# The gate product of the third head in the second mixer loop, moved behind its value products

## What is computed

```
def _mix(h, l, prm, past):
    proj = h @ prm['w_in'][l]
    hq, hf, hi, hg, sq, sk, sv, mx, mo, ga, gb, gc = jnp.split(proj, _in_split_points(), axis=-1)
    ...
    o_a, S_new = _hgrn2(hq, hf, hi, hg, lb, S0, prm['hg_gain'][l], hg_chunk)
    ...
        o_b = _sb_attend(q, jnp.concatenate([pk.astype(k.dtype), k], axis=1),
                         jnp.concatenate([pv.astype(v.dtype), v], axis=1),
                         P + jnp.arange(T), jnp.arange(P + T), sbb)
    ...
    o_c, (C_new, n_new, m_new, buf_new) = _mlstm(mx, mo, buf0, l, prm, C0, n0, m0, ml_chunk)
    merged = (jax.nn.sigmoid(ga.astype(f32)) * (o_a @ prm['w_hg_proj'][l])
              + jax.nn.sigmoid(gb.astype(f32)) * (o_b @ prm['w_sb_proj'][l])
              + jax.nn.sigmoid(gc.astype(f32)) * (o_c @ prm['w_ml_proj'][l]))
    y = (merged @ prm['w_out'][l]).astype(h.dtype)

def _mlstm_chunk(carry, inp):
    logD = b[:, :, None, :] - b[:, None, :, :] + it[:, None, :, :]
    m_t = jnp.maximum(b + m[:, None, :], jnp.max(logD, axis=2))
    Dm = jnp.exp(logD - m_t[:, :, None, :])
    W = jnp.einsum('bthd,bshd->btsh', q, k) * Dm
    numer = (inter[..., None] * jnp.einsum('bhvd,bthd->bthv', C, q)
             + jnp.einsum('btsh,bshv->bthv', W, v))
    denom = inter * jnp.einsum('bhd,bthd->bth', n, q) + jnp.sum(W, axis=2)
    ...
```

## Time and profile before

| | us |
|---|---|
| median of 3 runs | 1796.72 (1793.66 to 1801.37) |
| the profiled execution's own time | 1797.36 |
| its span | 1795.6 |
| TensorE busy | 1712.5 (95% of the span) |
| VectorE busy | 1035.5 (58%) |
| ScalarE busy | 789.3 (44%) |
| TensorE waiting for ACT L2017 at L1003 | 4.3 in two waits |
| TensorE waiting for pages at L757 | 1.6 (`pages`) and 1.1 (`ring`) |
| mean granted clock of TensorE | 0.984 |

### The profile page before, as it was taken

One profiled execution on the slowest core, in us unless ns is written; L12 is line 12 of the kernel. 1 busy time (PEld: TensorE's weight loads), 2 busy tenths in 40 slices (PEclk: granted clock), 3 DMA queues, 4 the chain that ended last, 5 costly groups with the idle time before them and its releaser, 6 DMA issues.

```text
span 1795.6 us, 33082 instructions
## 1 busy us (share of the span) xinstructions
PE 1712.5 (95%) x12604; PEld 1490.7 (83%) x12604; DVE 1035.5 (58%) x1874; ACT 789.3 (44%) x1430; POOL 71.1 (4%) x103
## 2 busy tenths in 40 slices
PE   5999999999999999999979999999999999999998
PEld 3898988878876687999969889788778766879997
DVE  3554545675567656655455554465665765566554
ACT  2554544445333315665345554353444331256552
POOL 0000000000000000000000000100000100000000
PEclk7999999999999999999999999999999999999999
DMA  8778565555557825555657784665464686455451
GB/s 340 260 260 329 210 224 205 183 209 220 190 210 259 314 97 210 186 176 205 253 194 277 268 334 170 234 227 185 148 241 154 236 316 218 143 210 187 171 219 56
DMA packets 85802, 391.81 MB, mean 218 GB/s; under 512 B 12328, under 2 KB 17712, under 8 KB 55344
## 3 DMA queue, kind: packets, MB, share of 16 engines
q1 hardware_dynamic: 72520, 368.15, 55.8%
q10 hardware_dynamic: 13160, 22.02, 3.5%
HBM read 377.30 MB, written 12.83 MB: 217 GB/s over the span
## 4 chain that ended last, share of the span: by engine, by line
PE 80%; DVE 9%; DMA 4%; ACT 3%; issue 2%; SPq 1%; ACTq 1%; POOL 0%; POOLq 0%; DVEq 0%
PE ps L594 17%; PE ps L589 15%; PE ps L590 15%; PE ps L550 10%; PE ps L776 3%; PE ps L794 3%; PE ps L793 3%; PE ps L570 2%; PE ps L740 2%; PE ps L658 1%; DMA pages<-in_k_pages 1%; PE ps L757 1%; PE ps L556 1%; DMA ring<-in_w_ffn_in 1%; DVE ring_parts L1137 1%
## 5 line engine op out<-in xcount | busy, mean ns | idle before, releaser
L1137 DVE TENSOR_TENSOR ring_parts<-ring,pages_parts 128x1024 fp32r<-128x1024 f32 (+1 forms) x288 | 334.0, 1193 | 158.9 <-ACT pages_parts L1753 158.8
L589 PE MATMUL ps<-arena_parts,pages_parts 128*128 128x264 f32 x1536 | 392.2, 290 | 18.3 <-DVE xn_parts L1225 10.2
L1753 ACT ACTIVATE pages_parts<-ring 128x1024 fp32r<-128x1024 f32 (+1 forms) x288 | 285.1, 1027 | 183.8 <-DMA ring<-in_w_ffn_in 55.7
L590 PE MATMUL ps<-xn_parts,pages_parts 128*128 128x264 f32 x1408 | 356.5, 287 | 0.0
L589 PEld LDWEIGHTS ps<-arena_parts,pages_parts 128*128 128x128 f32 x1536 | 294.3, 192 | 36.9 <-issue 30.5
L590 PEld LDWEIGHTS ps<-xn_parts,pages_parts 128*128 128x128 f32 x1408 | 268.9, 191 | 0.0
L594 PE MATMUL ps<-arena_parts,ring_parts 128*128 128x264 f32 x1536 | 225.7, 287 | 0.0
L550 PE MATMUL ps<-xn,ring 128*128 128x264 f32 x896 | 208.9, 389 | 0.6 <-ACT xn L1760 0.6
L594 PEld LDWEIGHTS ps<-arena_parts,ring_parts 128*128 128x128 f32 x1536 | 205.9, 190 | 0.0
L550 PEld LDWEIGHTS ps<-xn,ring 128*128 128x128 f32 x896 | 166.2, 190 | 34.9 <-ACT gates L1867 3.5
L590 PE MATMUL ps<-gates_parts,pages_parts 128*128 128x264 f32 x704 | 176.3, 285 | 0.0
(11 more groups left out here) (352 smaller groups left out, 2493.6 us busy)
## 6 DMA issues: line engine op xcount, KB each, us to landing
ring<-in_w_ffn_in SPq DMA_DIRECT2D x88, 1024.0 KB, 5.1
ring<-in_w_ada SPq DMA_DIRECT2D x32, 1536.0 KB, 6.5
ring<-in_w_a SPq DMA_DIRECT2D x32, 1536.0 KB, 6.9
ring<-in_w_ffn_down SPq DMA_DIRECT2D x32, 1408.0 KB, 6.2
pages<-in_k_pages SPq DMA_DIRECT2D x128, 256.0 KB, 6.0
ring<-in_w_ada SPq DMA_DIRECT2D x24, 1024.0 KB, 6.7
pages<-in_v_pages SPq DMA_DIRECT2D x88, 256.0 KB, 6.3
ring<-in_w_proj SPq DMA_DIRECT2D x8, 1536.0 KB, 8.2
```

Of the source, the lines that this page charges most:

```text
L589: mm(ps[:, b, 0:T], tile, hi[:, k, :], start=start, stop=False)
L590: return mm(ps[:, b, 0:T], tile, lo[:, k, :], start=False, stop=False)
L1137: v.tensor_tensor(ring_lo[:, r, at * P:(at + n) * P], w, whi[:, place, 0:n * P].bitcast(F32), ALU.subtract)\
L1753: A(whi[:, place, 0:n * P], ring[:, r, at * P:(at + n) * P], ACT.Copy).then_inc(S.whi_ready, 1)
```

## The change

The tuple that places the gate products changes for the third head (i = 2): product 5 moves from `FIRST_GATE` to `SECOND_GATE`, and the call for the first place gets the condition that the second had. ScalarE's program reads the same tuples, so its evacuation moves with it.

```
-FIRST_GATE, SECOND_GATE = (None, 3, 5, 6), (2, 4, None, 7)
+FIRST_GATE, SECOND_GATE = (None, 3, None, 6), (2, 4, 5, 7)
...
                 for i in range(HEADS):
                     if i:
                         key_rows(i)
-                        gslot = next_gate(FIRST_GATE[i], gslot)
+                        if FIRST_GATE[i]:
+                            gslot = next_gate(FIRST_GATE[i], gslot)
                         value_half(4 * i)
```

## The result

The changed kernel takes 1808.82 us (median of 4 runs, 1806.47 to 1809.04) against 1796.97 us before (4 runs, 1793.66 to 1801.37). The ratio is 1.0057, with a 95% interval of 1.0034 to 1.0081. Beside the experiments it was run again, and 9 to 12 us over the kernel before were expected: 1807.62 us, ratio 1.0059 (1.0040 to 1.0079). The forecast was 1801.4 us, the range ended at 1807. The sign of the forecast's sum was right, its size was half of what came.

What follows compares the result with a forecast made beforehand. TensorE, busy 1712.5 of 1795.6 us, was taken as the bound, so order matters only where it waits or its clock falls. Layer losses of 2.5 and 2.2 us (+4.7) on 1796.72 gave 1801.4 us, range 1796 to 1807.

Steps and rivals of the forecast that it cites:

- the queue: SyncE's queue: w_proj[1] waits for the gate product, half 12 starts 9.3 us after its issue; layers lose 2.5 and 2.2 us.
- The local part: TensorE, third head: gap before L1003 filled, but bare waits for pages and VectorE; first layer's head ends 0.7 us later.
- rival 1: Half 12's pages are in time, only TensorE's reordering counts: -1.7 us for both layers, 1795.0 us; 8%.
- The clock: TensorE's granted clock may fall behind the new waits, 1.5 us per fall; kept out of the sum, 28%.
- the rival with three falls: Far end of the 28% rival: one to three clock falls on TensorE give 1803 to 1806 us.
- the sign that the prediction itself had named for being wrong: Both layers' loops together change by less than 2 or more than 9 us.
- Rival 3: SyncE's queue: w_proj[1] and pages behind it move slowly (9.7 us), half 12 another 3.1 us later per layer, 1807.6 us; 10%.

Runs made afterwards that it cites:

- e3_held_proj: Kernel before, gate product in its old place, with w_proj[1] held until the third head's sum of squares (L1003): ratio 1.0052 to the kernel before.
- e1_late_proj: Changed kernel with w_proj[1] issued behind the pages of half 13 in place of half 11: ratio 0.9998 to the kernel before.
- e4_filled: Changed kernel with unread filler matmuls, 14 in front of half 8 and 20 in front of half 12: ratio 1.0050 to the kernel before.
- e4b_filled_short: Changed kernel with unread filler matmuls, 8 in front of half 8 and 11 in front of half 12: ratio 1.0037 to the kernel before.
- e6_both_late: Changed kernel with w_proj[0] issued behind the pages of half 8 and w_proj[1] behind those of half 13: ratio 0.9979 to the kernel before.

## Why the prediction was wrong

**What bounds the kernel, and the queue.** Right. That the gap before L1003 is filled and yet nothing is won, that w_proj[1] holds the pages of half 12 back, and that this is the main cost, is what the traces and e3_held_proj show. Its term was 9.3 us from issue to half 12. The runs have 9.30 and 9.39 us in the first layer and 9.96 and 10.03 us in the second: right, and 0.7 us short in the second layer.

**The local part.** Right in its sum, in the first layer partly by luck. Decay products 5.3 us (first layer) and 5.2 us (second) behind L1003 were forecast; they came at 4.81 and 5.32 us. In the first layer the waits were forecast as 0.9 us for pages and 1.8 us for VectorE and came as 1.89 and 0.27 us: half 8 came later than thought, and GpSimd's instruction began 2.4 us behind the second head's L1004, where it was 3.2 us behind L1003 before, so that VectorE was held up earlier and behind the wait for pages. In the second layer the wait for pages was 2.60 us, where 2.7 was forecast. The part on its own was priced in rival 1 at -0.8 and -0.9 us, and e1_late_proj has -0.8 and -0.9 us.

**The clock: the step that failed.** The sum left the falls of the clock out. The new waits were seen and their lengths too (2.7 and 3.3 us), but because the one old gap of 2.16 us had brought a fall in one layer and none in the other, the prediction called a fall a toss-up, made it a rival with 28%, and summed the forecast without any. That does not follow from its own reading: if each of three or four new waits of such a size is a toss-up, no fall at all has a chance of one in eight or less. In fact they came at the same three places in both profiles of the changed kernel: behind 3.26 and 3.35 us of waiting at half 12 in the first layer, behind 2.60 and 2.93 us at half 8 in the second, and behind 3.92 and 3.99 us at half 12 there. Only the wait of 1.89 (1.82) us at half 8 in the first layer brought none. The prices: 14.72 - 13.19 = 1.5 us behind half 12 in the first layer and 14.59 - 13.19 = 1.4 us in the second (both against the stretch in e4_filled and e4b_filled_short), and at the decay products 1480.36 - 1476.00 = 4.36 us to the query rows against 2.71 us before, 1.7 us. Together 4.6 us, where the sum had nothing.

The forecast's 4.7, the 4.6 us of the clock and the 0.7 us of the pages make 10.0 us; the two loops have 9.8 and 10.4. Layer by layer, and without the falls, the first lost 3.53 - 1.5 = 2.0 us (2.5 in the forecast) and the second 6.30 - 3.05 = 3.25 us (2.2 in the forecast). With 9.8 us for the two together, the sign that the prediction itself had named for being wrong, over 9 us, came. So the rival with three falls was what happened, priced about right at 1.5 us each and given too small a chance. The range ended at 1807 because it took three falls as its far end, and with that had no room for slower pages in the same run.

**The rivals.** Rival 3, slower transfers by 3.1 us in each layer, did not come: w_proj[1] took 6.5 and 7.2 us, not 9.7. Rival 1 needed pages that are not held, and e1_late_proj built just that.

**The chances.** Slower by over 0.5% had 8%. Both measurements lie at 0.57 and 0.59% with intervals from 0.34 to 0.81%, so on either side of that bound.

## What to carry to other kernels

When work moves on one engine, look for the load that waits for its end: a queue issues in order, so everything behind that load moves too, and here this cost 10 us where the move alone made no difference that could be measured. Give a new wait of TensorE like those here, of 2.6 to 4.1 us, the price of the half clock behind it in the sum itself and not in a rival, and ask before filling a gap whether the place that the work comes from can stand bare: with one load out of the way the move was worth nothing, and with both the kernel was 3.8 us faster. How far a load is moved matters too: two halves further back, that gain was gone.

## What was not expected of the hardware

- Over all kernels here the granted clock fell to half behind 11 of the 12 waits of 2.60 us and more in these loops; the exception is one of 3.15 us in e3_held_proj's second layer. A stretch at half clock had ended 2 us before that wait, but the wait of 3.04 us in its first layer had one 2.6 us before it, and there the clock fell again; why the two differ is open. Behind 2.37 us in e1_late_proj it did not fall. In e4b_filled_short it fell with no wait of note in the 9 us before. Of the old gap of 2.16 us before L1003 there are eight in the four kernels that keep it, and the clock fell behind four. So a wait of about 2 us may or may not cost 1.5 us more, with the same order of work.
- VectorE is held up by GpSimd for what is left of GpSimd's instruction: a tensor_scalar of 0.28 us took 1.92 us, a tensor_tensor of 0.43 us took 2.01 us. Both read SBUF alone. VectorE's instructions with an operand in PSUM were not held up: the tensor_tensor in front of the two tensor_scalars (L1602) took its usual 0.55 us at 581.58 us in the changed kernel, beside GpSimd's instruction from 581.33 to 583.42 us, and L1610 took 1.22 us in e6_both_late, within GpSimd's from 586.16 to 588.09 us.
- A filler matmul of 120 columns with its weight load, two records in the trace, took 0.23 us in a row of them.
